# The MLP's 1056 tokens in four PSUM banks of 264 in place of three banks of 352

## What is computed

```python
def rmsnorm(x, g):
    xf = x.astype(F32)
    y = xf * lax.rsqrt(jnp.mean(xf * xf, axis=-1, keepdims=True) + EPS)
    return (y * g.astype(F32)).astype(x.dtype)

def sq_relu_mlp(x, w_up, w_down):
    h = jax.nn.relu(x @ w_up)
    return (h * h) @ w_down
...
        x = x + sq_relu_mlp(rmsnorm(x, norm_ffn[l]), w_up[l], w_down[l])
```

## Time and profile before

| | |
|---|---|
| median of 3 runs | 2472.32 us (2471.91 to 2482.23) |
| profiled execution, its time | 2474.78 us |
| profiled execution, its span (first to last instruction) | 2473.0 us |
| mean granted TensorE clock | 0.988 of full speed |
| busy: PE / PEld / DVE / ACT / POOL | 2391.2 / 2287.6 / 1172.6 / 655.6 / 162.4 us |
| matmuls in the trace | 15530 |

### The profile page before, as it was taken

The page is one execution under the profiler, slowest core; times in us unless marked ns, Lnnn a source line. Parts: engine busy times, 40 slices in busy tenths (PEclk is TensorE's granted clock), DMA queues, the critical chain, the costliest instruction groups (busy, mean ns, idle before and its releaser), DMA issues.

```text
span 2473.0 us, 36951 instructions
## 1 busy us (share of the span) xinstructions
PE 2391.2 (97%) x15530; PEld 2287.6 (93%) x15530; DVE 1172.6 (47%) x2055; ACT 655.6 (27%) x1096; POOL 162.4 (7%) x208
## 2 busy tenths in 40 slices
PE   6899999988999999999999999999999999999998
PEld 6899898878999999999999877879999999999997
DVE  6545555568434334334336665566433333333333
ACT  3233222334212112112113454353212112112113
POOL 3000000013000000000002011012000000000002
PEclk8999999999999999999999999999999999999999
DMA  3212121101111111111112311101111111111111
GB/s 107 50 36 66 47 66 38 45 29 35 50 52 43 44 52 43 44 52 44 43 51 63 94 34 43 35 18 35 52 45 51 44 50 45 44 52 43 43 52 71
DMA packets 177416, 120.55 MB, mean 49 GB/s; under 512 B 23623, under 2 KB 173044, under 8 KB 177220
## 3 DMA queue, kind: packets, MB, share of 16 engines
q1 hardware_dynamic: 177108, 118.10, 16.3%
q10 hardware_dynamic: 144, 0.02, 0.0%
HBM read 110.94 MB, written 12.33 MB: 50 GB/s over the span
## 4 chain that ended last, share of the span: by engine, by line
PE 72%; issue 19%; DVE 4%; POOL 2%; ACT 1%; DMA 1%; SPq 0%; POOLq 0%; ACTq 0%; DVEq 0%
PE acc L1606 58%; PE acc L1888 3%; PE acc L1890 3%; PE acc L1889 3%; PE acc L1907 2%; PE acc L1930 1%; PE acc L1918 1%; POOL small L991 1%; DVE rstd L1054 1%; DVE w_lo L1036 1%; DVE x_res L1193 0%; DMA out_y_prompt<-y_out 0%; DVE q_t L1441 0%; DVE prob L1475 0%; POOL small L989 0%
## 5 line engine op out<-in xcount | busy, mean ns | idle before, releaser
L1606 PE MATMUL acc<-x_hi,w_hi 128*128 128x352 f32 x1560 | 506.7, 325 | 14.8 <-DVE x_lo L1042 6.4
L1606 PE MATMUL acc<-x_hi,w_lo 128*128 128x352 f32 x1560 | 502.0, 322 | 0.0
L1606 PE MATMUL acc<-x_lo,w_hi 128*128 128x352 f32 x1560 | 501.3, 321 | 0.0
L1606 PE MATMUL acc<-h_hi,w_hi 128*128 128x352 f32 x1536 | 495.4, 323 | 0.0
L1606 PE MATMUL acc<-h_lo,w_hi 128*128 128x352 f32 x1536 | 492.1, 320 | 0.0
L1606 PE MATMUL acc<-h_hi,w_lo 128*128 128x352 f32 x1536 | 491.9, 320 | 0.0
L1067 DVE TENSOR_TENSOR x_res<-x_res,acc 128x1056 f32<-128x1056 f32 x128 | 160.4, 1253 | 400.6 <-PE acc L1606 400.6
L688 ACT ACTIVATE w_hi<-w_raw 128x1024 fp32r<-128x1024 f32 x180 | 189.3, 1052 | 604.2 <-PE acc L1606 516.4
L1606 PEld LDWEIGHTS acc<-x_hi,w_hi 128*128 128x128 f32 x1560 | 293.6, 188 | 17.2 <-issue 11.7
L1606 PEld LDWEIGHTS acc<-x_lo,w_hi 128*128 128x128 f32 x1560 | 294.5, 189 | 0.9 <-issue 0.9
L1606 PEld LDWEIGHTS acc<-x_hi,w_lo 128*128 128x128 f32 x1560 | 294.1, 189 | 0.0
(11 more groups left out here) (265 smaller groups left out, 3087.5 us busy)
## 6 DMA issues: line engine op xcount, KB each, us to landing
w_raw<-in_w_up SPq DMA_DIRECT2D x64, 512.0 KB
w_raw<-in_w_down SPq DMA_DIRECT2D x64, 512.0 KB
w_raw<-in_w_mlstm_in SPq DMA_DIRECT2D x24, 512.0 KB
x_in<-in_x_prompt SPq DMA_DIRECT2D x8, 512.0 KB, 3.7
w_raw<-in_w_mlstm_out SPq DMA_DIRECT2D x8, 512.0 KB
w_raw<-in_w_q SPq DMA_DIRECT2D x16, 256.0 KB
w_raw<-in_w_attn_out SPq DMA_DIRECT2D x16, 256.0 KB
out_y_prompt<-y_out SPq DMA_DIRECT2D x8, 512.0 KB, 2.6
```

What stands on the lines that cost most here:

```text
L1606: last = T.matmul(out[:, b], w[:, k, m], x[:, TN * b:TN * b + TN], start=(k == 0 and i == 0), stop=(k == k_chunks - 1 and i == 2))
```

## The change

In the MLP a group becomes four banks, `MB` = 4, of `MN` = 264 columns each (4 x 264 = 1056). The two groups are then banks 0 to 3 and 4 to 7, in both layers: together all eight. `chunk` issues 12 matmuls of 264 columns where it issued 9 of 352; the first slab of the program, the mLSTM gates, stays at three banks. DVE's two readings go over 4 pieces of 264 columns. With all banks in use the sums of squares have to share banks with a group, so `sum_banks` and two waits change: PE waits with the second slab of an MLP until DVE has read the sums, and with the sums of the K/V norm until DVE has read the MLP's last group.

```diff
--- before.py
+++ after.py
@@ -27,6 +27,8 @@
 KD = D // P
 TB = 3
 TN = TOK // TB
+MB = 4
+MN = TOK // MB
 HEADS, DK, DV = 8, 64, 128
 NPAIR = HEADS // 2
 LC = 128
@@ -325,18 +327,15 @@
 
         def group(o):
             if o.const == 0 and o.index is None:
-                g = 0
-            elif o.const < O_MLP1:
-                g = 3 * (1 - o.parity)
-            else:
-                g = 4 * o.parity
-            return acc[:, g:g + 3, 0:TN]
+                return acc[:, 0:TB, 0:TN]
+            g = 4 * (1 - o.parity) if o.const < O_MLP1 else 4 * o.parity
+            return acc[:, g:g + MB, 0:MN]
 
         def sum_banks(no):
-            return (3, 7) if no == 3 else (6, 7)
-
-        def blocks(ap):
-            return ap.rearrange("p (t n) -> p t n", t=TB)
+            return (2, 3) if no == 3 else (6, 7)
+
+        def blocks(ap, t=MB):
+            return ap.rearrange("p (t n) -> p t n", t=t)
 
         def cols(t):
             return slice(t * P, t * P + (P if t < NCH else SAMP))
@@ -1099,9 +1098,9 @@
             def gate_inputs():
                 dve.wait_ge(rstd_ready, 1)
                 dve.wait_ge(out_ready, 1)
-                V.tensor_tensor(blocks(log_i[:]), group(At(0))[0:HEADS], blocks(rstd[0:HEADS]), ALU.mult).then_inc(dve_done, 1)
+                V.tensor_tensor(blocks(log_i[:], TB), group(At(0))[0:HEADS], blocks(rstd[0:HEADS], TB), ALU.mult).then_inc(dve_done, 1)
                 dve.wait_ge(dve_done, links.next)
-                V.tensor_tensor(blocks(gate_a[:]), group(At(0))[32:32 + HEADS], blocks(rstd[32:32 + HEADS]),
+                V.tensor_tensor(blocks(gate_a[:], TB), group(At(0))[32:32 + HEADS], blocks(rstd[32:32 + HEADS], TB),
                                 ALU.mult).then_inc(dve_done, 1)
                 dve.wait_ge(dve_done, links.next)
                 V.tensor_scalar(log_i[:], log_i[:], gate_bias[:, 0:1], None, ALU.add).then_inc(out_taken, 1)
@@ -1601,9 +1600,11 @@
                 out = group(o)
                 mh, ml = moving(k)
                 m = slice(P * n, P * n + P)
-                for b in range(TB):
+                first = o.const == 0 and o.index is None
+                nb, nn = (TB, TN) if first else (MB, MN)
+                for b in range(nb):
                     for i, (w, x) in enumerate(((hi, mh), (hi, ml), (lo, mh))):
-                        last = T.matmul(out[:, b], w[:, k, m], x[:, TN * b:TN * b + TN],
+                        last = T.matmul(out[:, b], w[:, k, m], x[:, nn * b:nn * b + nn],
                                         start=(k == 0 and i == 0), stop=(k == k_chunks - 1 and i == 2))
                 if k == k_chunks - 1:
                     last.then_inc(out_ready, 1)
@@ -1634,6 +1635,8 @@
                     if k == 4:
                         if no == 1:
                             pe.wait_ge(blk_taken, BLK0)
+                        if no == 2:
+                            pe.wait_ge(out_taken, O_KV)
                         if no == 3:
                             pe.wait_ge(blk_taken, BLK0 + TB * AFIRST[len(ATT)])
                         pe.wait_ge(ssq_ready, no + 1)
@@ -1844,6 +1847,8 @@
                         if first and c == 0:
                             slab(s, o, KD, normed, prepared(no), sum_squares(norm_no))
                         else:
+                            if first and c == 1:
+                                pe.wait_ge(ssum_taken, 2 * norm_no + 2)
                             slab(s + c, o + c, KD, normed)
 
                 def down(f, s, o, half):
```

## The result

The changed kernel takes 2502.19 us (median of 5, 2499.43 to 2504.10) against 2479.39 us of the kernel before (median of 5). The ratio is 1.0093, with a 95% interval of 1.0074 to 1.0111: slower by 0.93%, 23 us, clear of the 0.5%. The forecast was slower by 36.5 us and 1.5%. The kernel before has a median 7 us higher here than the 2472.32 from which the forecast was added up; from 2479.39 the same sum gives 2516.

The account below looks back on a forecast made before the run. TensorE's own pace, mostly the MLP's matmuls, was taken to bound the kernel. The terms 36.9 - 0.6 + 0.2 = +36.5 us on the median 2472.32 gave 2509 us, 1.5% slower, with a range from 2468 to 2565.

Parts of the forecast that it names:

- TensorE's pace is the time, banks are not waited for: Whole kernel: TensorE, busy 97% of the span, sets the time; a second full set of banks has nothing to win.
- 3072 more matmuls, each paying what isn't columns: MLP matmuls: 12288 of 264 columns replace 9216 of 352, so the part beyond columns is paid 4 times a pass, not 3.
- All of it is fixed: 122.1 ns: MLP matmul step: the 12.1 ns beyond columns stay whole at 264 columns, +12.0 ns per pass, +36.9 us.
- nearly proportional: Rival on the MLP matmul step: nearly all of the extra grows with the columns, 2472 to 2479 us; chance 0.20.
- Weight loads hidden at 112 ns: MLP matmuls: each weight load takes 112 ns beside the matmul before, under the expected 122, with 10 ns to spare.
- faster rival: Rival on the MLP matmul step: 264-column pieces go at the weight loads' pace, 112 ns, total 2387 us; chance 0.10.
- the cover's loss: MLP weight loads no longer hidden behind matmuls: every ns by which a load passes 122 costs 12.3 us.
- The larger fixed part by the reads' begins: Rival: 264-column reads begin at other addresses and the load's margin falls; steps 125 to 130 ns, 2545 to 2606 us; chance 0.20.
- Start of each MLP, -0.6 us, +0.2: TensorE's wait at the third slab for weights shrinks 0.3 us a layer, -0.6; longer chunks 4 and 5 delay the sum, +0.2.
- The added wait: Second slab of an MLP waits until VectorE has read the sums: costs nothing, since that read ends before TensorE arrives.
- Loop branches stay as they are: TensorE's stops at the MLP loop's branches, like DMAs and attention stages, were taken as unchanged, with no term in the sum.
- The stretches between the MLPs as long as they were: Sign for the profile after: the parts between the MLPs keep their length.

Follow-up runs that it names:

- layout_352: Changed kernel with three pieces of 352 columns in place of four of 264, new bank order and added waits kept: 2476.95 us against 2476.75, ratio 0.9997.
- unroll_264: Changed kernel with the MLP's three hardware-loop rounds written out on every engine: 2489.25 us, ratio 1.0047 to the kernel before.
- unroll_352: Kernel before with the MLP's three hardware-loop rounds written out on every engine: 2470.38 us, ratio 0.9978.
- start0_304: Kernel before with three pieces of 304 columns, all read from column 0 (less work, wrong values): 2302.37 us against 2480.26.
- start0_352: Kernel before with its three pieces of 352 columns all read from column 0 (wrong values): 2479.55 us against 2480.26.
- start0_512: Kernel before with three pieces of 512 columns, all read from column 0 (extra work, wrong values): 3125.33 us against 2480.26.
- layer1_264: Kernel with the change in the second MLP alone, the first keeping three pieces of 352 columns: 2490.07 us, ratio 1.0047 to the kernel before.

## Why the prediction was right, and which of its terms was off

The time came out in the range, and the direction and the main cause were right. By its own last sign ("wrong if the step at 264 columns isn't 122 ns") its size was not: the step is 120.8 ns, and the time rose by 22.8 us in place of 36.5. That 2509 stands only 7 us off the measured 2502 is in part luck, since the median that it starts from was 7 us below the one that 2502 is compared with.

- **TensorE's pace is the time, banks are not waited for.** Right: `layout_352` at 0.9997, no wait for a bank in either kernel.
- **3072 more matmuls, each paying what isn't columns.** Right in kind: all but 5 us of the loss is steps; half of the loss with the change in half of the MLPs, and none of it with three pieces in the new layout (0.9997).
- **"All of it is fixed: 122.1 ns", +36.9 us.** This is the term that was mis-sized: 120.8 ns, +18 to 21 us. The two rows that I took it by didn't carry it. That durations fall on a few values says nothing of how they grow with the columns, and these durations have modelled ends; the transposes also load 128 columns of weights each, whose pace alone was put at 112 ns, so their 108.6 doesn't single out a fixed part of 2; and that nothing is left over at half the pace holds as well for a read that keeps up with 1.2 but not quite with 2.4 columns per ns. At one begin, the four sizes show about 5 ns fixed and 0.441 ns a column. The truth lay about in the middle between my bounds, 0 and 36.9 us, and my "nearly proportional" rival was as near as the forecast for the step alone (119.6 with its 2 ns fixed).
- **Weight loads hidden at 112 ns.** Right: 176 and 240 columns both step at 0.11 us, and 264 is above it. The faster rival and the cover's loss are excluded by that.
- **The larger fixed part by the reads' begins.** The begin counts, but by 1% of a step (1 to 2 ns), not by the 3 to 8 of that rival.
- **Start of each MLP, -0.6 us, +0.2.** The wait came down by 0.4 us in all. The clock's lower level behind it, in one layer before and in both after, is +1.5 us in the profiled execution. It comes and goes at both sizes, so it can't be put down to the change by one execution; whether the change makes it more frequent, and what brings it, stays open.
- **The added wait.** Nothing, as said.
- **"Loop branches stay as they are."** Wrong, +5.0 us: the stops at four branches grew from 3.4 to 8.4 us. `unroll_264` and `unroll_352` show that it is the branches. That shorter matmuls make it worse is shown by `start0_304`, `start0_352` and `start0_512`, equal in all but the columns. `layer1_264` has it within one kernel: 1.8 us of stops in the layer of 352 columns, 4.0 in that of 264. Why is argued, not shown: if TensorE has a certain number of matmuls in hand while the branch's target is fetched, they cover less time when each is shorter.
- **"The stretches between the MLPs as long as they were."** 1.5 us longer in this execution, within what the kernels here differ by.

The two errors, 16 to 19 us too much in the steps and 5 too little at the branches, partly made up for one another.

## What to carry to other kernels

A cost that is seen at one size only can't be split into a fixed and a growing part by looking harder at it: keep both ends, and don't put half the chance on one. Cutting a pass of matmuls in more pieces is worth nothing where no bank is waited for, and it costs the fixed part once more per pass. When instructions on the bounding engine get shorter, ask what their length had been hiding: here the hardware loop's branches, and writing the loops out gave 0.46% and 0.22% back.

## What the runs showed of the hardware

- fp32r matmuls with their own 128-column weight load, at full clock and reads from one begin: 121.3, 139.2, 159.5 and 230.7 ns at 264, 304, 352 and 512 columns, about 0.441 ns a column plus 5 (one run each). At the lower clock 264 columns take 0.220 us and 352 take 0.294, which is the columns alone.
- Below some 243 columns (an estimate: where that line meets 112 ns) the weight load sets the pace: 0.11 us at 240, 176 and 32 columns.
- The begin of the moving operand in SBUF moved the step by 1%: 830 to 822 matmuls in 100 us, and 631 to 624.
- A branch back of a hardware loop stops TensorE in these kernels for 0.7 to 1.1 us at a step of 159 ns, for 1.4 to 1.8 at 121 (idle time of one stop, `before` and `after`) and not at all at 231. A second stop of 0.8 to 1.2 us can follow after some 15 more matmuls (after two of the four branches in `after`).
